# Four quarters of a layer norm, normalised in another order ahead of three projections

## What is computed

```python
for l in range(DEPTH):                       # 2
    ...
    mixed = jnp.concatenate([main, mem_out], axis=-1) @ w_out[l]
    x = layer_norm(DEEPNORM_ALPHA * x + mixed, ln_g[l, 0], ln_b[l, 0])
    ffn = peer_ffn(x, peer_wq[l], peer_subkeys[l], peer_u[l], peer_v[l])
    x = layer_norm(DEEPNORM_ALPHA * x + ffn, ln_g[l, 1], ln_b[l, 1])
```

## Time and profile before

| | |
|---|---|
| median of 3 runs | 3319.46 us (3316.66 to 3319.55) |
| the profiled execution | 3319.91 us, of which the span is 3318.1 us |
| TensorE busy | 3278.7 us (99% of the span) |
| VectorE busy | 2783.0 us (84%) |
| ScalarE busy | 1992.1 us (60%) |
| norm 0, first `centred` to the end of low(3) | 454.07 to 469.08 us |
| norm 1, the same | 1744.37 to 1761.11 us |
| norm 2, the same | 2015.68 to 2030.25 us |

### The profile page before, as it was taken

How to read it: one execution, slowest core, us unless ns; L and a number is a source line. 1 busy time by engine, 2 the same in 40 slices (tenths; PEclk the granted TensorE clock), 3 DMA queues, 4 the chain that set the end, 5 groups by cost and what they waited for, 6 DMA issues and landing times. The chain is left out here.

```text
span 3318.1 us, 52162 instructions
## 1 busy us (share of the span) xinstructions
PE 3278.7 (99%) x19468; PEld 2938.6 (89%) x19468; DVE 2783.0 (84%) x4030; ACT 1992.1 (60%) x3619; POOL 404.1 (12%) x262
## 2 busy tenths in 40 slices
PE   9999999999999999999999999999999999999998
PEld 8888889999999988888888887999999998888887
DVE  5775669999988888888887757999898888888887
ACT  4444555555888855555555545555688875555555
POOL 0000000011111112222200000011111112222220
PEclk9999999999999999999999999999999999999999
DMA  7553345788999999999974344578899989999995
GB/s 270 181 182 135 125 162 191 266 341 316 370 364 363 360 336 371 371 366 370 361 294 158 115 154 158 203 287 334 320 374 364 363 341 360 367 371 368 363 370 216
DMA packets 169221, 969.07 MB, mean 292 GB/s; under 512 B 18912, under 2 KB 52704, under 8 KB 55648
## 3 DMA queue, kind: packets, MB, share of 16 engines
q1 hardware_dynamic: 132192, 698.61, 55.4%
q0 software_dynamic: 36864, 268.45, 22.2%
HBM read 951.26 MB, written 15.73 MB: 291 GB/s over the span
## 5 line engine op out<-in xcount | busy, mean ns | idle before, releaser
L1693 DVE TENSOR_TENSOR wl<-raw,wh 128x1024 fp32r<-128x1024 f32 x1264 | 1523.9, 1219 | 421.8 <-ACT wh L584 419.1
L584 ACT ACTIVATE wh<-raw 128x1024 fp32r<-128x1024 f32 x1264 | 1334.0, 1058 | 769.8 <-PE ps L1023 682.3
L1023 PE MATMUL ps<-xx,wh 128*128 128x384 f32 (+1 forms) x5504 | 1709.1, 373 | 14.0 <-DVE wl L1693 5.8
L1023 PE MATMUL ps<-xx,wl 128*128 128x192 f32 (+1 forms) x5504 | 1420.7, 258 | 0.0
L1023 PE MATMUL ps<-wh,act 128*128 128x512 f32 x3584 | 1188.8, 389 | 0.2
L1023 PEld LDWEIGHTS ps<-xx,wh 128*128 128x128 f32 x5504 | 1034.1, 188 | 88.6 <-DVE wl L1693 16.7
L1023 PEld LDWEIGHTS ps<-xx,wl 128*128 128x128 f32 x5504 | 1048.6, 191 | 0.5
L1023 PE MATMUL ps<-wl,act 128*128 128x512 f32 x2304 | 896.4, 389 | 0.0
L1023 PEld LDWEIGHTS ps<-wh,act 128*128 128x128 f32 x3584 | 672.8, 188 | 141.0 <-DVE wl L1693 1.0
L1023 PEld LDWEIGHTS ps<-wl,act 128*128 128x128 f32 x2304 | 432.5, 188 | 89.4
L1667 POOL DMA_INDIRECT arena<-in_urows,idx x128 | 151.5, 1184 | 2006.7 <-DVE idx L1951 1130.7
(11 more groups left out here) (219 smaller groups left out, 1560.4 us busy)
## 6 DMA issues: line engine op xcount, KB each, us to landing
raw<-in_u SPq DMA_DIRECT2D x256, 1024.0 KB
raw<-in_v SPq DMA_DIRECT2D x256, 1024.0 KB
raw<-in_w SPq DMA_DIRECT2D x118, 1024.0 KB
h_scratch<-hring SPq DMA_DIRECT2D x128, 96.0 KB
hring<-h_scratch SPq DMA_DIRECT2D x128, 96.0 KB
arena<-in_memT SPq DMA_DIRECT2D x4, 512.0 KB, 6.9
raw<-in_w SPq DMA_DIRECT2D x4, 512.0 KB, 9.2
arena<-in_xT SPq DMA_DIRECT2D x4, 512.0 KB, 9.0
```

Of the source, the lines that this page charges most:

```text
L584: nc.scalar.activation(wh[:, j, :], raw_piece(p), ACT.Copy).then_inc(hi_ready, 1)
L1023: return nc.tensor.matmul(out, lhs, rhs, start=start, stop=stop, **kw)
L1693: v.tensor_tensor(wl[:, j, :], raw_piece(p), wh[:, j, :].bitcast(F32), ALU.subtract).then_inc(lo_ready, 1)
```

## The change

In norms 0, 1 and 2 only two quarters are normalised before quarter 0 is turned, scaled and split. The third is normalised behind that, and the fourth next (on VectorE with low(0) between them). Quarter 1 is then split (`high(1)`, `low_quarter(..., 1)`) before quarter 2 is scaled. On TensorE the transposes of quarter 2 move from ahead of the first product to between groups (0, 0) and (0, 1), and those of quarter 3 from there to the start of group (1, 0), behind its wait for low(1). Norm 3 keeps its order. No instruction is added or removed.

```diff
 # ScalarE
-            for q in range(3):
-                centred(q)
+            centred(0)
+            centred(1)
+            if n == 3:
+                centred(2)
             turned(0)
             if n < 3:
                 high(0)
+                centred(2)
             centred(3)
             turned(1)
+            if n < 3:
+                high(1)
             turned(2)
             if n < 3:
-                high(1)
                 high(2)
                 hi(p_next + 2, 2)
                 hi(p_next + 3, 3)
 # TensorE, first_pair
-            for q in range(3):
+            for q in range(2):
                 turn(n, q)
             pe.wait_ge(evac_done, t0)
...
                     if s == 0:
                         pe.wait_ge(x_ready, x_from + q + 1)
                     if q == 0 and s == 1:
+                        turn(n, 2)
+                        pe.wait_ge(xta_ready, 8 * n + 4)
+                    if q == 1 and s == 0:
                         turn(n, 3)
-                        pe.wait_ge(xta_ready, 8 * n + 4)
 # VectorE
-            for q in range(3):
-                centred(q)
+            centred(0)
+            centred(1)
+            if n == 3:
+                centred(2)
             if n == 1:
                 lo(p_next, 0)
             turned(0)
-            centred(3)
             if n < 3:
+                centred(2)
                 low_quarter(xt, n + 2, 0)
             if n == 1:
                 lo(p_next + 1, 1)
+            centred(3)
             turned(1)
+            if n < 3:
+                low_quarter(xt, n + 2, 1)
             turned(2)
             if n < 3:
-                low_quarter(xt, n + 2, 1)
                 low_quarter(xt, n + 2, 2)
                 lo(p_next + 2, 2)
             turned(3)
```

## The result

| | before | after |
|---|---|---|
| median of 11 runs each, alternating | 3318.22 us | 3327.38 us (3324.35 to 3329.04) |
| ratio, after to before | | 1.0024, interval 1.0016 to 1.0031 |
| the profiled execution | 3319.91 us | 3327.38 us |
| its span | 3318.1 us | 3325.6 us |

The change makes the kernel slower by 0.24%, some 8 us (0.0024 x 3318); the interval reaches from 5.3 to 10.3 us. The two medians differ by 9.16 us and the profiled pair by 7.47. One run of the kernel before took 4002.6 us, and one of experiment 1 13699.23 us; they stand in no ratio, and the others of the kernel before lie between 3316.25 and 3320.45.

The account below looks back on a forecast made before the run. TensorE bounds the kernel, but at the norms it waits for the VectorE and ScalarE chain. Norms 0, 1, 2 cost 2.8 + 2.3 + 1.3 = 6.4 on 3319.91, giving 3326.3 us, range 3321.5 to 3329.5.

Parts of the forecast that it names:

- Low(0) earlier by 0, 0.7 and 0.1 us: Front of norms 0, 1, 2: one centred fewer ahead of turned(0) gains nothing, 0.68 and 0.11 us.
- The chain in series: VectorE and ScalarE behind low(0): low(1) at +4.05 (norm 1 +5.19), low(2) 3.33 later, low(3) ending 5.70 after that.
- Ends of low(3): Norms 0, 1, 2: low(3) ends 17.8, 19.0 and 17.5 us after the first centred instead of 15.0, 16.7 and 14.6.
- The hand-over prices: Between VectorE and ScalarE around each high part: 0.09 us over and 0.03 us back, bounds +-0.3 us a norm.
- the estimate from the Trainium skill's rule: Access overhead at the two new alternations: 0.15 us of overlap lost each, 0.9 us over three norms.
- SP's queue: Behind low(3) in norm 0: keys issued 2.8 us later, and the already late fourth slab 2.82 later, without spare.
- The new waits ahead of the transposes of quarter 3: TensorE, group (1, 0): it waits for low(1) and only then turns quarter 3, 0.79 us that stood in cover before.
- norm 2's 1.3: Loss at norm 2: 2044.36 against 2043.09, only 1.3 us since TensorE was late before; up to 2.9 otherwise.
- Rival 1: The change pays at the front: only the low(0) gains 0.68 + 0.11 count, 3319.1 us; chance 0.04.
- Rival 2: Half is absorbed: low clock on products before hides the new waits, together near 4 us, 3323 to 3324; chance 0.18.
- Rival 3: The clock: longer TensorE idling puts low clock on products, 1.6 us a norm, 3327.9 to 3329.5; chance 0.14.

Follow-up runs that it names:

- experiment 1: Kernel before, with only high(1) and low(1) moved ahead of turned(2) on ScalarE and VectorE: 3324.25 us, ratio 1.0011.
- experiment 4: The changed kernel run again with no edit: 3327.10 us, ratio 1.0019 to the kernel before.
- experiment 12: The changed kernel run a third time with no edit: 3326.84 us, ratio 1.0023 to the kernel before.
- experiment 8: Kernel before, with centred(2) moved behind turned(0) in norm 1 alone, on VectorE alone: 3318.26 us, ratio 0.9998.
- experiment 2: Kernel before, with only the new order of centred on both engines: 3321.04 us, ratio 1.0003.
- experiment 9: Changed kernel, with twelve more small products on TensorE between the 16 transposes and the first product: 3325.92 us, ratio 1.0019 to the kernel before.
- experiment 11: Changed kernel, with TensorE's order as before (24 transposes ahead of the first product): 3325.86 us, ratio 1.0021 to the kernel before.
- experiment 10: Kernel before, with only TensorE's new order plus twelve small products ahead of the first product: 3330.46 us, ratio 1.0032.
- experiment 7: Changed kernel, with centred(3) on VectorE ahead of low(0) instead of behind it: 3326.76 us, ratio 1.0018 to the kernel before.

## Why the prediction was right

Forecast 3326.3 us, measured 3327.38 both as median and in the profiled execution. That the two lie so close is in part luck. The forecast stood on the profiled execution of before, which lay 1.7 us above the median of its eleven runs (3319.91 against 3318.22). As a difference the forecast was 6.4 us, where the three comparisons of the kernel after (the first, and experiments 4 and 12) give 6.3 to 8.0 by their ratios, and the medians of the first 9.16. Point by point:

- **Low(0) earlier by 0, 0.7 and 0.1 us.** Counted from `centred(0)` it starts at 5.14, 4.74 and 5.11 us in the profile after, before at 4.75, 5.47 and 4.33. Norm 1 is right. In norms 0 and 2 it came 0.4 and 0.8 later than before, since half clock lay on the transposes of quarters 0 and 1. In the other two profiles it did not lie on quarter 0, and low(0) started at 4.26 in both norms. For norm 0 I had taken the slow transposes of one profile for a fixed pace. But the 0.5 us that norm 0 seems to gain there is the clock's: with these transposes at full clock the order before has low(0) at 4.33 as well (norm 0 of experiments 1 and 8), so the change itself gives 0.07. In norm 1 it came at 5.18 in the other two, a gain of 0.3. The clock moves this term by up to 0.9 us.
- **The chain in series.** Low(1) 4.05, 5.19 and 4.05 us behind low(0): measured 4.04, 5.17 and 4.04. Low(2) 3.33 behind low(1): 3.37, 3.32 and 3.32 (3.6 in norms 0 and 2 of the repetitions, where TensorE turned quarter 2 late). Low(3) ends 5.70 behind the start of low(2): 5.68 in norm 0, 5.68 and 5.69 in the others. The gaps ahead of low(1) and low(2) were to be 1.2 to 1.3 us and are 1.18 to 1.19; VectorE's idle time ahead of the low parts in norm 0 is 0.46 + 1.19 + 1.18 = 2.83 us ("about 3").
- **Ends of low(3)** at 17.8, 19.0 and 17.5: measured 18.23, 18.91 and 18.16 here, 17.6, 19.3 and 17.6 in the two repetitions.
- **The hand-over prices** (0.09 and 0.03 us) held to 0.01: the gap is 0.09 + 1.06 + 0.03. By the estimate from the Trainium skill's rule on the overhead of each operation ("Perfetto Trace Analysis", section "Optimizing Scalar/DVE Operations") 0.9 us would have come on top. The trace has such a loss of overlap, but inside the sum: the rows of single operations hold it already (two low parts together 2.36 us, each alone 1.23). No step at full clock is longer than its sum.
- **SP's queue.** The keys are issued at 472.87 instead of 469.11, 3.22 later counted from the first `centred` (forecast 2.8), and that the fourth slab had no spare held: in norm 2 after, and in five of the six norms 0 and 2 of the three profiles of the kernel after, the scores start 1.86 or 1.87 us after that slab's first high part. The sixth, norm 0 of the first profile, is TensorE's own lateness, 0.26 us past that point (480.99 + 1.87 = 482.86, the scores at 483.11).
- **TensorE behind the turns.** The new waits ahead of the transposes of quarter 3 did not come. These transposes start at 466.47, low(1) ended at 465.02, and no idle time stands ahead of them: half clock on the eight turns of quarter 2 (1.91 us) and the products around them had used the wait up. Of the signs listed this one failed outright, and it cost nothing; the times of low(0) and low(3) in norms 0 and 2 missed by up to 0.9 and 0.7 us.
- **The mis-sized term is norm 2's 1.3.** The pair gave 1.81, since low(3) ended 18.16 us after the first `centred` instead of the 17.5 forecast: the low clock once more, on the turns of quarter 0. And the base of that term hung on one execution: 26.77 us with the low clock on products, 25.09 without, 26.57 with it again in experiment 8. With no low clock on products, as in the second profile of before, the norm costs 28.1 - 25.1 = 3.0, close to the 2.9 that stood as the upper bound. Norm 0 measured 2.92 (forecast 2.8) and norm 1 2.20 (2.3).
- **Rival 1**, the gain at the front: the front did gain in experiments 2 and 8, by 0.7 and 0.5 us in norm 1, and only the second kept it. With the chain in series it is lost.
- **Rival 2**, half absorbed: it needs executions before with the low clock on products. It is commoner than one profile showed: of the six norms 0 and 2 with the order of before (both profiles of before, and experiment 8) three had it, at 26.53 to 26.77 us against 25.09 to 26.06 for the others. So a part of the loss is absorbed in many executions, but not half. The three comparisons of the kernel after (1.0024, 1.0019, 1.0023, so +6.3 to +8.0 us) lie well above its 4.
- **Rival 3**, the clock. Its condition came true, its price did not. Mean granted clock over 20 us from the first `centred`, TensorE, kernel after; over the same stretches before it was 0.91 each time.
```profile
454.61:474.61 20.00, 16.93 (x89) 0.83 0.04 9
1747.28:1767.28 20.00, 17.02 (x85) 0.74 0.16 54
2020.93:2040.93 20.00, 17.14 (x89) 0.83 0.05 10
```
A mean of 0.83 is (1 - 0.83) x 20 / 0.5 = 6.8 us at the lower level, twice the 3.4 of before, and 0.74 is some 10.2 us. I had argued that the new waits were too short for that; the stretches came all the same. The loss lies beside VectorE's: at group (2, 1) TensorE comes just when VectorE has the weights (471.61 against 471.56), and in experiment 4 it still waits 0.23 us there. In norm 1 all three profiles of the kernel after have 10.2 us of it, and norm 1 costs 2.2 to 2.7 against the 2.3 of the sum. The upper values are the profiles in which half clock lay on the turns of quarter 0 and low(0) came at 5.18 instead of 4.74, so there the clock is worth some 0.4.

That the low clock costs the changed kernel next to nothing is read from those waits. It was not shown by a version of it that ran without: experiment 9 was meant to be one and did not shorten the low clock.

That the loss of norms 0 and 2 goes by the keys and the fourth slab is read from the traces too. No run moved their issue ahead of low(3), so it stays open how much would be left if they came early, with TensorE still waiting for the weights of group (2, 1). In norm 1, where four slabs are ahead, 2.2 to 2.7 us are lost without them.

## What to carry to other kernels

When two engines hand pieces to each other in strict order, bringing one piece forward can split a pair that hid the hand-over: here each split put 1.18 us of the other engine's work in series, twice a norm, where 0.40 us of idle time had stood once, and `centred(3)`, which had filled the wait for `high(0)`, came onto the path with 0.72 more, for at most 0.7 us gained at the front in one norm. Ask which piece has the second customer (here the last, with SP's queue and the fourth slab behind it) before an earlier first piece is paid for with a later last one. And parts of a reordering are to be costed together: one engine's half alone cost at least as much (9.7 us, interval 5.0 to 12.0) as the whole on the same chip (7.1, interval 3.3 to 9.3).

## What the runs showed of the hardware

- Two profiles of the same kernel have TensorE's granted clock low at different places of a norm, and this alone moves a norm by 1.7 us (norm 2 before, 26.77 and 25.09) and the start of `turned(0)` by 0.9 us. A term of that size from one profile is an accident until a second shows it.
- The stretch at the lower level in a norm was 3.4 us in both profiles of before and 3.4 to 10.2 us with sixteen transposes ahead of the first product instead of 24. The number of transposes alone does not decide it: experiments 2 and 11 have 24, the last eight behind an idle time for the later `centred(2)` (1.20 us in norm 0 of experiment 11), and 3.4 to 6.8 us. Experiment 9 has twelve more small products in that wait and the long stretch all the same (10.2 us in norm 1), experiment 10 has them and a short one in norms 0 and 1 (3.4 us). What decides between them stays open.
- Three of the fourteen profiles show another stretch at the lower level, in the attention between norms 1 and 2. The same stretches of experiment 11 and of experiment 4; the columns are length, busy time of the five engines, clock, DMA share, GB/s:
```profile
1920.00:1924.00 4.00, 4.00 (x31) 3.87 (x29) 3.05 (x10) 3.09 (x15) 0.00 (x0) 0.79 0.00 0
1924.00:1928.00 4.00, 4.00 (x25) 3.25 (x23) 2.65 (x4) 2.57 (x3) 0.00 (x0) 0.50 0.14 18
```
```profile
1920.00:1924.00 4.00, 4.00 (x34) 3.89 (x35) 3.05 (x10) 3.65 (x17) 0.00 (x0) 1.00 0.00 0
1924.00:1928.00 4.00, 3.80 (x40) 2.76 (x39) 3.62 (x6) 3.69 (x8) 0.00 (x0) 1.00 0.02 6
```
TensorE did small products and transposes before it fell, with idle times of 0.43, 0.63 and 0.58 us in the nine us before and none in the last 2.7. Experiment 4 has nearly the same idle times at this place, and its clock stayed up. From the first row sum of norm 1 to the first `centred` of norm 2 experiment 11 took 2.6 us more than experiment 4 (255.46 against 252.86), experiment 10 the same, and experiment 7 3.8. Why the clock fell there is open too.
- The granted clock came back while TensorE did nothing but transposes. In norm 0 before it did the 24 of the earlier trace rows from 455.02 to 459.52, behind 2.75 us of idle time, and nothing else. Two stretches of this:
```profile
455.46:458.88 3.42, 3.42 (x18) 3.42 (x17) 2.62 (x6) 2.90 (x6) 0.00 (x0) 0.50 0.00 0
458.88:459.50 0.62, 0.62 (x6) 0.41 (x4) 0.62 (x1) 0.62 (x2) 0.00 (x0) 1.00 0.00 0
```
By the Trainium skill, "TensorE: Matmul & The Clock Gate", section "Part 4: PE-mode transpose", transposes do not count as activity that brings the full clock. This trace does not agree, and norm 1 before shows the same (0.50 from 1745.70 to 1749.12, then 1.00). Nor do transposes as such run at the slow pace: in experiment 12 sixteen of norm 0 took 1.97 us behind 2.75 us of idle time, in the first profile of the kernel after the same sixteen took 3.45.
